# Asking earlier for three weight pieces in a two-block transformer kernel on one Trainium2 core

## The reference, cut to what matters

```python
def first_block(x, ...):                   # a gated delta rule and an mLSTM side by side, then:
    x = x + y @ w_out[l]
    h2 = _rmsnorm(x, norm2_g[l])
    x = x + _peer(h2, peer_wq[l], peer_keys[l], peer_u[l], peer_v[l])
    return _rmsnorm(x, normf_g)

def _peer(h, w_q, sub_keys, u_tab, v_tab):
    ...                                    # top 16 of 16384 rows for each of 8 heads and each token: idx, gate
        u = u_tab[ib]                      # gathers 128 rows of 1024 f32 for each token
        act = gelu(einsum("td,thkd->thk", tb, u))
        vv = v_tab[ib]                     # and 128 rows of the second table
        return einsum("thk,thkd->td", gb * act, vv)

def second_block(x, c, ctx, ...):
    for i in range(2):                     # layer 0: pooling mixer, layer 1: attention; each with a conv FFN
        ...
        x = x + g1 * mixer(h, hc)          # layer 0's pooling uses pool_w (1 MB), the same for x and for ctx
        x = x + g2 * _conv_ffn(...)        # ffn_w_up (11 pieces of 2 MB), ffn_w_down (6 pieces)
        if need_ctx_out:                   # layer 0 also runs on the 256 context tokens, with the same weights
            ctx_s = ctx_s + cg1 * y_c
            ctx_s = ctx_s + cg2 * _conv_ffn(...)
```

## The kernel before

| load | slot | waits for |
|---|---|---|
| down pieces 3, 4, 5 of the context | 0, 1, 2 | `p_cd` 4, 8, 12 |
| `kvc`, weights of the context's keys and values (2048 KB) | 0 | `p_cd` 24, then `p_cd` 16 |
| `pool`, weights of the pooling for x (1024 KB) | 0 | `p_v` 248, and `p_ckv` 3 |
| `up` 0 and `up` 1 of layer 0 for x (2048 KB each) | 1, 2 | `p_cd` 20 and 24 |
| `up` 2 | 0 | `p_pl` 4, the end of the pooling product |

## Time and profile before

### The profile page before, as it was taken

How to read it: one execution, slowest core, us unless ns; L and a number is a source line. 1 busy time by engine, 2 the same in 40 slices (tenths; PEclk the granted TensorE clock), 3 DMA queues, 4 the chain that set the end, 5 groups by cost and what they waited for, 6 DMA issues and landing times.

```text
span 1667.6 us, 22193 instructions
## 1 busy us (share of the span) xinstructions
PE 1478.8 (89%) x8310; PEld 1059.6 (64%) x8310; DVE 1106.1 (66%) x2162; ACT 583.5 (35%) x847; POOL 824.9 (49%) x746
## 2 busy tenths in 40 slices
PE   8999999766565699999888885889999999999999
PEld 7997675654221266665443441438999896799987
DVE  4865633798488877877756675417886557468864
ACT  6653331211121222221100001127665454466652
POOL 0025230376767765656667777742675113036640
PEclk9999999987977899999799997999999999999999
DMA  7447860598999999999999999994555545635551
GB/s 281 152 151 301 318 253 26 210 389 304 393 407 371 409 401 402 402 403 403 401 401 394 409 396 402 406 396 161 171 187 190 189 182 222 243 111 202 176 191 38
DMA packets 154252, 477.15 MB, mean 286 GB/s; under 512 B 10017, under 2 KB 12321, under 8 KB 150945
## 3 DMA queue, kind: packets, MB, share of 16 engines
q0 software_dynamic: 73728, 268.47, 41.2%
q1 hardware_dynamic: 80416, 207.27, 34.0%
HBM read 474.65 MB, written 1.05 MB: 285 GB/s over the span
## 4 chain that ended last, share of the span: by engine, by line
PE 54%; DMA 13%; DVE 11%; POOL 10%; issue 5%; ACT 2%; DVEq 0%; ACTq 0%; POOLq 0%
PE ps L673 53%; DMA arena<-in_peer_v,cl 11%; POOL arena L2802 8%; DVE arena L1851 2%; PE ps L677 1%; POOL wring L2802 1%; DVE arena L1466 1%; DMA wring<-in_peer_v,cl 1%; DVE arena L1472 1%; DVE wring L1851 1%; DMA wring<-in_peer_u,arena 1%; DVE arena L1469 0%; DVE cvb L1472 0%; DVE arena L1781 0%; ACT arena L2190 0%
## 5 line engine op out<-in xcount | busy, mean ns | idle before, releaser
L673 PE MATMUL ps<-arena,wring 128*128 128x256 f32 (+2 forms) x2360 | 596.0, 488 | 106.0 <-DMA arena<-in_peer_v,cl 101.2
L673 PEld LDWEIGHTS ps<-arena,wring 128*128 128x128 f32 (+1 forms) x2360 | 333.0, 168 | 352.7 <-DMA arena<-in_peer_v,cl 179.7
L1851 DVE CUSTOM_DVE_ANT_0 arena<-arena 128x1024 f32<-128x1024 f32 x214 | 257.6, 1226 | 134.8 <-DMA arena<-in_peer_u,arena 131.9
L2802 POOL DMA_INDIRECT arena<-in_peer_u,arena x214 | 240.0, 1121 | 192.4 <-DVE arena L1809 78.2
L2802 POOL DMA_INDIRECT arena<-in_peer_v,cl x214 | 229.2, 1071 | 77.3 <-issue 60.4
L673 PE MATMUL ps<-hhl,wh 128*128 128x256 f32 (+1 forms) x1056 | 252.4, 323 | 1.2 <-POOL hhl L2812 0.7
L2190 ACT ACT_TABLE_LOAD x64 | 82.1, 1283 | 392.9 <-DVE arena L1851 266.1
L1466 DVE TENSOR_TENSOR wl<-wring,wh 128x2048 fp32r<-128x2048 f32 (+1 forms) x76 | 168.1, 2212 | 60.0 <-ACT wh L2193 58.2
L673 PE MATMUL ps<-hhl,wl 128*128 128x256 f32 x704 | 198.7, 282 | 0.0
L673 PEld LDWEIGHTS ps<-hhl,wh 128*128 128x128 f32 x1056 | 175.8, 190 | 19.5 <-POOL hhl L2812 2.5
L2193 ACT ACTIVATE wh<-wring 128x2048 fp32r<-128x2048 f32 (+1 forms) x78 | 146.1, 1874 | 70.7 <-PE ps L673 68.9
(11 more groups left out here) (257 smaller groups left out, 2025.4 us busy)
## 6 DMA issues: line engine op xcount, KB each, us to landing
wring<-in_ups SPq DMA_DIRECT2D x33, 2048.0 KB, 9.2
wring<-in_ada SPq DMA_DIRECT2D x24, 2048.0 KB, 9.9
wring<-in_ffn_w_down SPq DMA_DIRECT2D x12, 2048.0 KB, 9.0
wring<-in_w_in SPq DMA_DIRECT2D x8, 2048.0 KB, 8.3
wring<-in_ffn_w_down SPq DMA_DIRECT2D x6, 1536.0 KB, 7.6
wring<-in_peer_wq SPq DMA_DIRECT2D x4, 2048.0 KB, 16.1
wring<-in_attn_w_qkv SPq DMA_DIRECT2D x4, 2048.0 KB, 8.4
wring<-in_w_out SPq DMA_DIRECT2D x2, 2048.0 KB, 9.7
```

Of the source, the lines that this page charges most:

```text
L673: return pe.matmul(o, l, r, start=start, stop=stop)
L1851: ve.tensor_tensor_reduce(out=o, in0=o, in1=h2[:, t, :], scale=1.0, scalar=0.0, op0=MUL, op1=ADD, accum_out=dots[j % 2][:, k:k + 1]).then_ ...
L2802: po.indirect_dma_start(out=ring[n % NR], out_offset=None, in_=table, in_offset=bass.IndirectOffsetOnAxis(ap=which, axis=0)).then_inc(S[f" ...
```

## The change

The load of `kvc` moves ahead of the wait for `p_cd` 24 and of the two loads behind it. `pool` and `up` 0 are asked for right behind those two, ahead of the wait for `p_v` 248; `up` 1 and the rest stay behind that wait. The restart of the rotation (`nth[0] = 0`) is gone, so `pool` now takes slot 1, `up` 0 slot 2, `up` 1 slot 0 and `up` 2 slot 1.

```diff
+        load("kvc", ("p_ckv", 3), kcols(a["attn_w_qkv_2"][0], 1024, 512), n=3)
         sp.wait_ge(*at("p_cd", 24))
         sp.dma_start(hpC[:, 0:1568], a["c_bands"]).then_inc(S["d_l"], 16)
         sp.dma_start(nfb, a["normf_g"].partition_broadcast(128)).then_inc(S["d_g2"], 16)
-        load("kvc", ("p_ckv", 3), kcols(a["attn_w_qkv_2"][0], 1024, 512), n=3)
-        nth[0] = 0
+        load("pool", ("p_pl", 4), pool_w(), n=3)
+        load(("up", 0, 0), split_done(1), up(0, 0), n=3)
         sp.wait_ge(*at("p_v", 248))
-        load("pool", ("p_pl", 4), pool_w(), n=3)
 
         def ffn_loads(l, n0):
-            for g in range(11):
+            for g in range(1 if l == 0 else 0, 11):
                 load(("up", l, g), split_done(n0 + 2 * g + 1), up(l, g), n=3)
```

## The result

The changed kernel took 1680.51 us (median of 4 runs, 1676.87 to 1681.45) against 1671.05 us for the kernel before (median of 4, 1670.04 to 1671.52). The ratio is 1.0053 with a 95% interval of 1.0037 to 1.0069: 6.2 to 11.5 us slower. The forecast was 1679.6 us.

A forecast was written before the change was run, and what follows sets the result against it. DMA engines full with gathers until the last one lands were taken as the bound. +8.0 (`pool`, `up` 0) + 1.0 (`kvc` burst) - 0.5 (end) + 0 (earlier landing) = +8.5 on 1671.1: 1679.6 us, range 1674 to 1684.

The forecast's parts named there:

- What bounds the stage: Last part of the gather stage: it ends when full DMA engines have moved all gathers plus loads served ahead, 408 GB/s.
- the hidden room: Refuting sign, 935 to 995 us: spare DMA rate in before, seen as gathers whose landing did not slow beside `kvc`.
- `pool` and `up` 0, +8.0: Ahead of the last gathers: 3.146 MB in full engines cost the 7.7 us floor and a little, 8.0 us.
- The higher prices of 9.3 and 10.1: Upper bounds in us for `pool` and `up` 0, from gathers missing beside earlier bursts, 2.96 and 3.2 us per MB.
- `kvc`, +1.0 for a burst of its own: Near 935 us, ahead of the bands: its bytes cancel, a separate burst costs 0 to 1.7 us, taken as 1.0.
- The end of the gathers, a gain of 0.5: Last eight v rows: only `up` 1 asked for beside them, relief between 0 and 1.4 us, taken as 0.5.
- Nothing gained behind the gathers: After the last gather: nothing waits for the pieces that come earlier, `up` 0 had 5.7 us of slack; gain 0.
- The signs: Expected in the new trace: request times, rate of 400 GB/s or more, longer v-row waits, last v row near 1126 us.
- "Swallowed": 935 to 995 us: PE, not DMA, sets the pace and catches up part; slower by only 3 to 6 us; chance 0.17.
- ride along free: Gathers bound by something else, added bytes cost nothing, end relieved: 1669.7 us, or 1671.1 if not; chance 0.07.
- "Worse than additive": v-row waits lower TensorE's clock, delaying ring release and gathers: 12 us and more, 1683 to 1686; chance 0.07.

The follow-up runs named there:

- The 2 MB that nobody reads: The kernel before with one more 2 MB load behind `kvc` into a free slot, nothing moved: 1685.63 against 1681.39 us, ratio 1.0022.
- the fourth trace: Against the unchanged kernel before: `pool` and `up` 0 early, `up` 1 held until the last v row, `kvc` behind the bands: 1675.85 us, ratio 1.0047.
- the third set: Runs beside each other: kernel before unchanged (median 1668.59 us), changed kernel (1678.44), and two with `up` 1 held until the last v row (1676.45, 1675.85).
- the last two lines of the table: `pool` and `up` 0 early, `up` 1 held until the last v row, against before: with `kvc` early 1676.45 us, with `kvc` behind the bands 1675.85.
- the two sets with `kvc` alone: The kernel before with only `kvc` moved ahead of the wait for `p_cd` 24, run twice: ratios 1.0002 and 1.0010.
- the run made for it: The kernel before with `up` 0 asked for ahead of `pool` at `p_v` 248: ratio 1.0003, interval 0.9985 to 1.0021.
- The `up`-1-held kernel: The changed kernel with `up` 1 and the rest held until `p_v` 256: 1682.42 against 1681.15 us for before, ratio 1.0002; later 1676.45 us, ratio 1.0051.
- the second set: Against before (1681.15 us): `kvc` alone early 1.0010, `pool` and `up` 0 alone early 1.0039, changed with `up` 1 held 1.0002, `up` 0 ahead of `pool` 1.0003.

## Why the prediction was right, and where not

**What bounds the stage: right.** The stage ends when the engines have moved the gathers and whatever stands ahead of the last one. POOL's 41 gathers for 46 at the same 407 to 408 GB/s say so, and so do the landings beside `kvc`, 14 us in place of 9: the hidden room that would have refuted the prediction was not there in these traces. The 2 MB that nobody reads fit, but their interval holds zero.

**`pool` and `up` 0, +8.0: right.** The clean measure is the fourth trace against the first: 72.4 - 64.8 = 7.6 us from the bands to the full-width products, for a floor of 7.7. Up to the rows behind the 248th the same two traces differ by 8.2 us, and from the first trace of before (66.0) the 7.6 would be 6.4, so the size is known to about 1 us. The higher prices of 9.3 and 10.1, which came from charging a whole burst's loss to its bytes, were too high for loads that join a burst.

**`kvc`, +1.0 for a burst of its own: its bytes moved as forecast, the price of the burst is not shown.** 0.6 us by the medians of the third set, not told apart from zero nor from 1.0. In the traces its 2.1 MB went from one side of the bands' request to the other: +3.6 us and -3.6 us between the last two lines of the table. Between the first profile pair the first of these stretches grew by 7.0 us (96.7 against 89.7), more than the 5.1 us of the bytes, between the pair of the third set by 5.1; one execution each does not tell this from scatter, and the two sets with `kvc` alone only bound the whole at -1.3 to +4.2 us, where both intervals overlap.

**The end of the gathers, a gain of 0.5: wrong.** This is the term "I take a gain of 0.5". It was a loss of 1.1 us: from the rows behind the 248th to the last pair 10.1 us in the changed kernel against 9.1 before, in both pairs of traces, against 7.6 with nothing beside it. That the plain loads slow the last rows was right (1.5 us before, for a forecast 1.4); the step that failed is what a change of these loads does. The prediction had thought that fewer bytes asked for must hurt the last gathers less. Before, 5.2 MB were asked for there with `pool` first and cost 1.5 us; in the changed kernel 2.1 MB of `up` 1 alone cost 2.6 us. The Trainium skill's rule that an engine takes turns packet by packet (DMA: Bandwidth & Descriptors, "Queues, rings and completion order"), quoted in the prediction for a loss, named the right sign; the size of about 1 us came from the rows at 995 us. That it is the length of the pieces is not shown: the run made for it asked too late, and so the cause of this loss stays open.

**Nothing gained behind the gathers: right.** 25.65 and 25.64 us from the last rows to the FFN.

**The signs.** Four of those that the prediction names did not come. The wait behind the bands was to be longer than 10.6 us and was 9.15; the added waiting stands in later rows. The rate was to be 400 GB/s or more throughout and was 387 from 995 to 1040 us (393 before in the same stretch). The last spacing was to stay under 3.9 us and was 4.09. The last pair was to start near 1126 and did at 1123.82, because this execution had been 3.3 us ahead.

**The rivals.** "Swallowed" and "ride along free" fall in the first timing and in the third set (at least +6.2 and +8.3 us). The `up`-1-held kernel of the second set, at most +3.4 us where the third set gave +7.9, shows that the price is not the same under every condition. There the first rival has something for it. From 935 to 995 us the three traces of the first two sets with `kvc` ahead of the bands have 396 to 407 GB/s, the five without 346 to 372, where the first timing and the third set have 407 to 409 with it or without. First row the kernel with `up` 0 first, which is before itself up to the wait for the 248th row, second the one with `up` 1 held, both of the second set:

```profile
935.00:995.00 60.00, 53.14 (x203) 26.59 (x204) 41.61 (x103) 6.37 (x10) 41.98 (x42) 0.97 0.98 372
```

```profile
935.00:995.00 60.00, 50.83 (x191) 24.60 (x192) 39.34 (x96) 6.36 (x10) 43.48 (x41) 0.94 1.02 397
```

So there was room ahead of the bands in those sets, by an estimate from these rates as much as the bytes of `kvc` (some 39 GB/s over 60 us, 2.3 MB). From the last down piece to the rows behind the 248th these two traces need 207.9 and 213.0 us, 5.1 more, where in the third set before and the same kernel differ by 8.7. With `kvc`'s 5.1 us for nothing the `up`-1-held kernel would come to 8.0 - 1.5 - 5.1 = +1.4 us, and `pool` and `up` 0 without `kvc` would stay at their full price, near what was measured. But then `kvc` alone should have been some 5 us faster than before, and both sets exclude that (-3.5 and -1.3 us at the lowest). Why the price was lower there stays open.

"Worse than additive" is not needed, since the terms add up. But PE's clock was not always as before: over the stretch of the long waits it was 0.83 against 0.81 (995 to 1040 us), behind it 0.73 against 0.90 (1040 to 1075 us) in the first pair and 0.71 against 0.78 in the third set. The time from the full-width products to row 249 shows nothing of it (46.8 and 47.0 us).

The sum came out near because two terms leaned against each other: the end was 1.6 us dearer than forecast, `kvc` and the bytes 0.8 us cheaper, and +8.5 stands against +9.5 and +9.85. So the mechanism was right for the larger part, and some of the nearness is luck.

## What to carry to other kernels

Where the DMA engines are full up to the point that releases the next stage, as here, a load asked for earlier costs about its bytes over the rate. It pays only if somebody waits for it behind that point, so first look whether the piece's first reader ever waited. A hold on plain loads near the end of a stream of gathers is best judged by the spacing of the last uses, not by the megabytes that are asked for: here 2.1 MB cost more than 5.2 MB.

## What the runs showed of the hardware that was not expected

- One plain load of 2.1 MB beside the last gathers delayed the last pair by 2.6 us, three loads of 5.2 MB with the shorter rows first by 1.5 us (10.1 and 9.1 us from the rows behind the 248th to the last pair, against 7.6 with none).
- Beside one plain load of 2.1 MB the gathers took 14 us from issue to landing in place of 9, at the same 407 to 408 GB/s.
- SP passed the wait for the 248th row about 6 us late in several traces of the first two sets (1125.97 against 1119.93), and at once in the traces of the first timing and of the third set. PE's weight loads stood still for nothing shown for 168 to 192 us in the first two sets and 146 to 155 in the others. What either waited for no run tested.
- The same kernel gave a median of 1681 us in two sets and 1669 to 1671 in the first timing and the third set; the second and the third set ran on the same chip. Effects under 1% were settled only by kernels run beside each other where the times of before lay within 5.3 us.
